# One decoder layer on one core: where the attention probabilities' word planes are split and joined, and in which order two weight chunks are multiplied

## The reference, cut to what matters

```
proj = h @ w_in                              # q, k, v of MoBA; q, k, v, r of GLA; a low-rank gate
p = softmax(q k^T * scale - slope * distance)          # MoBA, 8 heads x 64, causal, one block
moba_o = p @ v
o = chunked gated linear attention(qg, kg, vg, log_a)  # GLA, 4 heads, key 64, value 128
gla_o = rmsnorm(o) * gla_norm_g * silu(rg)             # rg: the output gate
mix = concat(moba_o, gla_o) @ w_mix_o
x = LN1(alpha * x + mix)
x = LN2(alpha * x + CrossAttn(x, mem))       # keys and values of mem from w_xkv
x = LN3(alpha * x + W2 relu(W1 x)^2)
```

## Time and profile before

| | us |
|---|---|
| median of 3 runs | 400.91 (400.53 to 401.12) |
| the profiled execution: its time | 399.95 |
| its span, first to last instruction | 398.0 |
| PE busy in the span | 387.2 (97%) |
| DVE busy | 354.3 (89%) |
| ACT busy | 260.3 (65%) |
| POOL busy | 100.4 (25%) |
| mean granted TensorE clock | 0.997 of full speed |

### The profile page before, as it was taken

One profiled execution on the slowest core, in us unless ns is written; L12 is line 12 of the kernel. 1 busy time (PEld: TensorE's weight loads), 2 busy tenths in 40 slices (PEclk: granted clock), 3 DMA queues, 4 the chain that ended last, 5 costly groups with the idle time before them and its releaser, 6 DMA issues.

```text
span 398.0 us, 5609 instructions
## 1 busy us (share of the span) xinstructions
PE 387.2 (97%) x2068; PEld 329.1 (83%) x2068; DVE 354.3 (89%) x450; ACT 260.3 (65%) x341; POOL 100.4 (25%) x87
## 2 busy tenths in 40 slices
PE   8999999978999999999999999999999999999995
PEld 5888888867888888898988888888888888888883
DVE  5599596999998787878798888999999999999997
ACT  6667578524745645547585548788877777888751
POOL 2059344856882202200102500000000000000003
PEclk9999999999999999999999999999999999999998
DMA  8997739493773274364818556767777777776202
GB/s 290 376 357 260 253 111 245 134 352 102 248 276 113 101 246 178 116 215 172 260 38 308 198 176 184 212 195 240 234 221 235 238 230 230 233 228 182 75 2 105
DMA packets 31585, 81.27 MB, mean 204 GB/s; under 512 B 8038, under 2 KB 9670, under 8 KB 27462
## 3 DMA queue, kind: packets, MB, share of 16 engines
q1 hardware_dynamic: 28720, 76.39, 57.1%
q0 software_dynamic: 2160, 3.93, 5.7%
q10 hardware_dynamic: 678, 0.59, 0.5%
HBM read 78.28 MB, written 1.05 MB: 199 GB/s over the span
## 4 chain that ended last, share of the span: by engine, by line
PE 69%; DVE 1%; issue 0%; DVEq 0%
PE bank L1705 14%; PE bank L1706 14%; PE bank L1707 13%; PE bank L2078 13%; PE bank L2085 7%; PE bank L1764 4%; PE bank L1768 2%; PE bank L1711 1%; PE bank L1891 1%; PE bank L1957 0%; PE bank L2006 0%; DVE stats L1650 0%; DVE X L1659 0%; PE bank L2164 0%; PE bank L1956 0%
## 5 line engine op out<-in xcount | busy, mean ns | idle before, releaser
L1110 DVE TENSOR_TENSOR w_lo<-raw,w_hi 128x2048 fp32r<-128x2048 f32 x30 | 72.7, 2430 | 5.9 <-ACT w_hi L692 5.9
L692 ACT CAST w_hi<-raw 128x2048 fp32r<-128x2048 f32 x32 | 60.7, 1912 | 16.2 <-PE bank L1707 11.1
L2078 PE MATMUL bank<-actA,w_hi 128*128 128x512 f32 x224 | 55.4, 390 | 0.0
L655 POOL DMA_DIRECT2D raw<-in_w_ff x15 | 13.2, 877 | 155.6 <-DMA raw<-in_w_ff 155.6
L2078 PEld LDWEIGHTS bank<-actA,w_hi 128*128 128x128 f32 x224 | 42.0, 188 | 8.7
L1705 PE MATMUL bank<-w_hi,actB 128*128 128x512 f32 x107 | 42.6, 398 | 0.0
L1706 PE MATMUL bank<-w_lo,actB 128*128 128x512 f32 x107 | 41.8, 391 | 0.0
L1707 PE MATMUL bank<-w_hi,actB 128*128 128x512 f32 x107 | 41.8, 390 | 0.0
L1764 PE MATMUL bank<-actA,w_hi 128*128 128x512 f32 x156 | 38.3, 392 | 0.0
L1705 PE MATMUL bank<-w_hi,actA 128*128 128x512 f32 x96 | 37.9, 395 | 0.0
L1707 PE MATMUL bank<-w_hi,actA 128*128 128x512 f32 x96 | 37.4, 390 | 0.0
(11 more groups left out here) (254 smaller groups left out, 889.1 us busy)
## 6 DMA issues: line engine op xcount, KB each, us to landing
raw<-in_w_ff SPq DMA_DIRECT2D x32, 1024.0 KB, 5.4
raw<-in_w_in SPq DMA_DIRECT2D x10, 1024.0 KB, 6.3
raw<-in_w_xkv SPq DMA_DIRECT2D x8, 1024.0 KB, 6.8
raw<-in_w_mix_o SPq DMA_DIRECT2D x4, 1024.0 KB, 4.9
raw<-in_w_xq SPq DMA_DIRECT2D x4, 1024.0 KB, 5.0
raw<-in_w_xo SPq DMA_DIRECT2D x4, 1024.0 KB, 5.5
raw<-in_w_ff POOLq DMA_DIRECT2D x15, 256.0 KB, 5.0
raw<-in_lead SPq DMA_DIRECT2D x6, 384.0 KB, 5.3
```

The costliest lines, as they stand in the source:

```text
L655: pool.dma_start(half_view(u)[:, 1536:2048], w_ff2[q, :, 512:1024], accum_op=ALU.add)\
L692: act.copy(dst, half_view(u)).then_inc(hi_done, 1)
L1110: dve.tensor_tensor(dst, half_view(u), hi_part.bitcast(f32), ALU.subtract).then_inc(lo_done, 1)
L2078: pe.matmul(b[:, :].rearrange("p (h s) -> p h s", h=2), hi[:, k, m * P:(m + 1) * P], actA[:, :, k, :], start=k == 0, stop=False, skip_grou ...
```

## The change

It has three parts.

1. POOL makes all four splits in a row, and the four joins move to ACT. SP issues the second, third and fourth turn directly behind each other, and unit (7, 0), unit (7, 1) and then X behind them; before, X stood behind the second turn and unit (7, 0) between the third and the fourth.
2. The output gate's columns become chunk 4 and GLA's values chunk 5. `rg0` and `rg1` are multiplied first. `exp_r(0)` stands between the exponentials of the softmax, `silu(0)` ahead of the last four norms on DVE; `silu(1)` keeps its place. `vg0` takes bank 5 as before and `vg1` bank 4 in place of 1.
3. On ACT the casts of both halves of chunk 5 stand in a row, and so do their low parts on DVE.

```
 CHUNKS = [ ...
-    ("w_in", "cols", VG), ("w_in", "cols", RG),
+    ("w_in", "cols", RG), ("w_in", "cols", VG),
 ...
-    + ... + [("va1", 4), ("vg0", 5), ("vg1", 1)]
-    + [("rg0", 2), ("diag", 0), ("rg1", 3), ("xk00", 0), ("xk01", 1), ("pv0", 6), ("pv1", 7)]
+    + ... + [("va1", 4)]
+    + [("rg0", 2), ("rg1", 3), ("vg0", 5), ("diag", 0), ("vg1", 4), ("xk00", 0), ("xk01", 1), ("pv0", 6), ("pv1", 7)]
 ...
-CHUNK_END = {..., 4: "vg1", 5: "rg1", ...}
+CHUNK_END = {..., 4: "rg1", 5: "vg1", ...}
 @@ sync
             load(unit(6, 0), chunk_source(6, 0), 4)
             turn_planes(0)
             load(unit(6, 1), chunk_source(6, 1), 4)
-            turn_planes(1)
+            for j in range(1, HA // 2):
+                turn_planes(j)
+            load_chunk(7)
             sp.dma_start(X[:], ...).then_inc(x_in, 16)
-            turn_planes(2)
-            load(unit(7, 0), chunk_source(7, 0), 4)
-            turn_planes(3)
-            load(unit(7, 1), chunk_source(7, 1), 4)
 @@ gpsimd
-            make_planes(0)
-            make_planes(1)
-            join_planes(0)
-            join_planes(1)
-            make_planes(2)
-            make_planes(3)
+            for j in range(HA // 2):
+                make_planes(j)
             wait_full(pool, "diag")
             pool.memset(lev_q[1], 0.0).then_inc(lev_q_zeroed, 1)
-            join_planes(2)
-            join_planes(3)
 @@ scalar
+            def join_planes(j):
+                act.wait_ge(turned_in[j], 16)
+                act.copy(by_word(planes[j]), by_plane(probs_words[j])).then_inc(probsT_made, 1)
 ...
             hi_half(5, 0)
-            evacuate("vg0", vg[:, 0, :])
+            hi_half(5, 1)
             exps(4)
             exps(5)
-            hi_half(5, 1)
+            exp_r(0)
             exps(6)
             exps(7)
-            evacuate("vg1", vg[:, 1, :])
+            exp_r(1)
             hi(MEM_UNIT, actB_hi[:].rearrange("p a s -> p (a s)"))
+            join_planes(0)
             hi_half(6, 0)
-            exp_r(0)
+            join_planes(1)
+            evacuate("vg0", vg[:, 0, :])
             b = wait_full(act, "diag")
             act.copy(diag[:], b[:, 0:8]).then_inc(freed("diag"), 1)
             hi_half(6, 1)
             decay(0)
-            exp_r(1)
+            join_planes(2)
+            evacuate("vg1", vg[:, 1, :])
+            join_planes(3)
+            decay(1)
             hi_half(7, 0)
-            decay(1)
             hi_half(7, 1)
 @@ vector
             lo_half(5, 0)
-            norm(4)
-            norm(5)
             lo_half(5, 1)
-            norm(6)
-            norm(7)
+            silu(0)
+            for h in range(4, HA):
+                norm(h)
 ...
             exponents(0)
             lo_half(6, 0)
             lo_half(6, 1)
-            silu(0)
             exponents(1)
             silu(1)
 @@ tensor
-            tokens(4, 0, A, "vg0")
-            tokens(4, 1, A, "vg1")
-            tokens(5, 0, A, "rg0")
+            tokens(4, 0, A, "rg0")
+            tokens(4, 1, A, "rg1")
+            tokens(5, 0, A, "vg0")
             b = begin("diag")
 ...
-            tokens(5, 1, A, "rg1")
+            tokens(5, 1, A, "vg1")
```

More of the change, by code:

```diff
@@ L168 @@
      ("ka0", 1), ("ka1", 2), ("ka2", 3), ("ka3", 0), ("va0", 2)]
-    + [(f"score{h}", b) for h, b in enumerate((4, 5, 6, 7, 1, 3, 0, 2))] + [("va1", 4), ("vg0", 5), ("vg1", 1)]
[1 row of a table removed]
+    + [(f"score{h}", b) for h, b in enumerate((4, 5, 6, 7, 1, 3, 0, 2))] + [("va1", 4)]
[1 row of a table added]
     + [("lv0", 4), ("lv1", 5), ("xk10", 2), ("xk11", 3), ("xk20", 0), ("lv2", 6), ("xk21", 1), ("lv3", 7),
@@ L184 @@
     FILL[_name] = (_bank, sum(b == _bank for b, _ in FILL.values()))
-CHUNK_END = {0: "kg1", 1: "qa3", 2: "ka3", 3: "va1", 4: "vg1", 5: "rg1", 6: "xk11", 7: "xk31", 8: "xv01",
+CHUNK_END = {0: "kg1", 1: "qa3", 2: "ka3", 3: "va1", 4: "rg1", 5: "vg1", 6: "xk11", 7: "xk31", 8: "xv01",
              10: "mo11", 11: "xv11", 12: "xq11", 13: "xq31", 15: "xo11", C_FF1_0: "hid1"}
@@ L579, in make_planes @@
                 pool.tensor_copy(by_plane(planes[j]), by_word(probs_words[j])).then_inc(planes_made, 1)
-            def join_planes(j):
-                pool.wait_ge(turned_in[j], 16)
-                pool.tensor_copy(by_word(planes[j]), by_plane(probs_words[j])).then_inc(probsT_made, 1)
-            make_planes(0)
-            make_planes(1)
-            join_planes(0)
-            join_planes(1)
-            make_planes(2)
-            make_planes(3)
+            for j in range(HA // 2):
+                make_planes(j)
             wait_full(pool, "diag")
             pool.memset(lev_q[1], 0.0).then_inc(lev_q_zeroed, 1)
-            join_planes(2)
-            join_planes(3)
             pool.wait_ge(lev_q_zeroed, 2)
@@ L755, in exps, with exp_r @@
                                    accum_out=sums[:, 2 * h + t:2 * h + t + 1]).then_inc(exp_done, 1)
+            def exp_r(t):
+                b = wait_full(act, f"rg{t}")
+                act.activation(sg[:, t, :], b[:, :], ACT.Exp, scale=-1.0).then_inc(expr_done, 1)
+            def join_planes(j):
+                act.wait_ge(turned_in[j], 16)
+                act.copy(by_word(planes[j]), by_plane(probs_words[j])).then_inc(probsT_made, 1)
             hi_half(4, 0)
@@ L765, in _ @@
             hi_half(5, 0)
-            evacuate("vg0", vg[:, 0, :])
+            hi_half(5, 1)
             exps(4)
             exps(5)
-            hi_half(5, 1)
+            exp_r(0)
             exps(6)
             exps(7)
-            evacuate("vg1", vg[:, 1, :])
+            exp_r(1)
             hi(MEM_UNIT, actB_hi[:].rearrange("p a s -> p (a s)"))
+            join_planes(0)
             hi_half(6, 0)
-            def exp_r(t):
-                b = wait_full(act, f"rg{t}")
-                act.activation(sg[:, t, :], b[:, :], ACT.Exp, scale=-1.0).then_inc(expr_done, 1)
-            exp_r(0)
+            join_planes(1)
+            evacuate("vg0", vg[:, 0, :])
             b = wait_full(act, "diag")
@@ L1201, in _, with silu @@
             lo_half(5, 0)
-            norm(4)
-            norm(5)
             lo_half(5, 1)
-            norm(6)
-            norm(7)
+            def silu(t):
+                dve.wait_ge(expr_done, t + 1)
+                v = sg[:, t, :]
+                link(dve.tensor_scalar(v, v, 1.0, None, ALU.add))
+                link(dve.reciprocal(v, v))
+                b = wait_full(dve, f"rg{t}")
+                dve.tensor_tensor(v, v, b[:, :], ALU.mult).then_inc(freed(f"rg{t}"), 1)
+            silu(0)
+            for h in range(4, HA):
+                norm(h)
             def exponents(n):
@@ L1256, in masked @@
                     b[:, :].rearrange("p (a b w) -> p a b w", a=8, w=w)).then_inc(freed(name), 1)
[L1258 to L1264, removed]
             def mix(n, name):
```

## The result

| | before | after |
|---|---|---|
| median | 400.88 us (400.53 to 401.12, 4 runs) | 395.03 us (394.53 to 395.20, 4 runs) |
| ratio, 95% interval | | 0.9853 (0.9836 to 0.9870) |
| profiled execution: time, span | 399.95, 398.0 us | 394.53, 392.6 us |
| its mean granted clock | 0.997 | 1.000 |

The account below looks back on a forecast made before the run. PE was taken to bound the kernel, with 4.8 us of waits before 102 us; 0.3 + 2.1 + 1.5 + 0.2 = 4.1, plus 0.2 for refills, gave 400.91 - 4.3 = 396.6 us, range 395.4 to 399.3.

Parts of the forecast that it names:

- What bounds it: PE bounds the kernel; its waits of 4.8 us before 102 us, plus some tenths for refills, are the most to gain.
- the first: Rival: all PE waits go, DVE gets its 4.4 us and locks back without new ones; 395.9 us, chance 0.13.
- the late turns of the others: Fourth turn late: rival 2, 7.6 us turn plus a lock, 398.6 us, chance 0.21; rival 4, far later, 402.8, 0.06.
- The last join: PE's 2.08 us wait for the last join before pv goes, with 2.9 us to spare.
- The size of a join: A join on ACT takes 1.4 us, from a cast's time by the element; the skill's estimate was 1.47 us.
- The lock: A POOL copy holds DVE for its length; moving joins gives DVE back about 1.9, 1.7 and 0.7 us.
- Level 1: PE's 1.54 us wait for POOL's part of level 1 goes, with 0.7 us to spare, the tightest place.
- The low parts: PE's wait for (6, 1) shrinks from 0.44 to 0.1 us, for (7, 1) from 0.73 to 0.5.
- The queue and X: X behind chunk 7 on SP delays chunk 8's units by 2.8 us, at no cost; X is read after 113.
- the banks: New banks for vg0 and vg1, read out later, cost nothing; 1.9 us of cover at the first.
- The waits and the refills: PE's waits give 0.3 + 2.1 + 1.5 + 0.2 = 4.1 us, pipeline refills beside them 0.2.
- The step that failed: Final step: the median's 0.96 us above the profiled execution is carried over, giving 400.91 - 4.3 = 396.6 us.

Follow-up runs that it names:

- the runs on one chip: The changed kernel again, unchanged, 394.93 us, and the kernel before with only part 1 of the change, 395.77 us, timed on the same chip.
- the changed kernel with the slow start: The changed kernel run once more, unchanged: 395.91 us, ratio 0.9855 to the kernel before.
- the second trace of the kernel before: Trace of the kernel before run once more, unchanged: 400.71 us, ratio 0.9990.
- the filled kernel: The kernel before with ten idle products between level 0 and level 1 on PE: 400.76 us, ratio 0.9991.

## Why the prediction was right in kind and short in size

- **What bounds it: right.** PE gained where it had waited, and after 102 us no new wait stands. Of the rivals the first came nearest in time (395.9), but by luck: its mechanism, all waits gone and no new lock, didn't come. A wait of 0.66 is left and both late splits met DVE's work. None of the late turns of the others came.
- **The last join: right.** The 2.08 us went, with 2.2 us of cover where 2.9 were forecast. The size of a join was wrong (1.95 us, not 1.4), which used only idle time of ACT. The estimate of 1.47 us from the Trainium skill was nearly as far off (ScalarE: Activation LUTs, "What ACT_TABLE_LOAD costs"); the page gives its figure for fp32 and bf16, and these are 16-bit integers.
- **The lock: right, and it is the whole matter.** With the joins on POOL the gain is zero. The fourth split met the subtraction as stepped through.
- **Level 1: right.** No wait is left, with 1.0 us to spare where 0.7 was forecast: `decay(1)` at 82.81, 84.3 forecast.
- **The low parts: right.** A wait of 0.66 us at 96.5, forecast 0.5 at 97.1 (the start is 0.8 earlier).
- **The queue and X: the cost of nothing was right**, and so was it for the banks.
- **Parts 2 and 3: small.** By the runs on one chip, 0.84 us on top of part 1, which gives the rest. The prediction didn't split them.
- **The waits and the refills.** Of the sum's terms the waits came as forecast, 4.13 us against 4.1. The refills were mis-sized: 0.5 us, not 0.2, with the three waits that went (0.44, 2.08 and 1.54).
- **The step that failed: "The median of the runs is 0.96 above that execution, so I forecast 400.91 - 4.3 = 396.6."** It takes the one traced execution for a typical one and carries its distance from the median over to the changed kernel. There the distance is 0.50 (395.03 - 394.53), and the traced execution also had the luck of a fast start. Of the miss of 1.57 us, 0.34 is the stretch (4.64 against 4.3, the refills), and the remaining 1.2 is this step.

Where the excess was, the marks show. A kernel's median less the mark to end of its trace is what stands ahead of the first mark and behind the last product. In 12 of the other 13 traces that is 45.0 to 45.6 us, and in one (the changed kernel with the slow start) 46.5. In the trace that the forecast was read from it is 46.75 (400.88 - 354.13), though its first mark at 39.59 is itself a late one. So this execution ran some 1.2 us faster between the marks than the kernel before usually does. It is an estimate, since it takes the other traces for typical. The excess lay in the stretch, and the change takes it away: by the second trace of the kernel before the stretch gains 5.60 us of the 5.85.

What it is made of, the runs show in part. In the execution traced first, PE's 4.8 us of waits came in pieces, the longest 2.08, and the clock held. In the second trace 4.12 of them came in one piece, the clock fell, and the stretch was 0.96 us longer. But most of the 0.96 was there before the fall: level 1 began at 92.2 us in both, though the second trace had passed the first mark 0.78 us earlier (38.81 against 39.59), so the fast start gained nothing there. What the fall cost behind it came mostly in place of the wait of 0.73 for the low part of (7, 1) and its refill, which the second trace doesn't have. Over the 71 executions of the kernel before in the three sets the mean granted clock is 0.989 to 0.999 with a mean of 0.993, lower than the 0.997 of the first trace in all but one; the changed kernel's 13 runs have 0.997 to 1.000. So the execution that I read was an unusual one by its clock too, and the change takes away the long waits behind the low clock. What stays open is how much of the median's excess is the clock. Over the 71 the time hardly follows the clock (those at 0.995 and above have a median of 401.06 us, those at 0.993 and below 400.98), and filling the wait raised the clock and not the speed. It may be that an execution without a fall pays in longer waits, as the traced one of the filled kernel did; that is argued, not shown.

## What to carry to other kernels

Here a copy on GpSimd beside a full VectorE cost VectorE its whole length, and on an engine with idle time it cost nothing, even at the same duration; look for such copies before moving products or transfers about. When the profiled execution is faster than the median and its mean clock higher than that of the other runs, it may not be a typical one: a gain worked out from it can leave out what waits cost in the others, and the range must reach below. Compare two traces from a mark behind the start, or chance at the start is read as gain.

## What the hardware did that I had not expected

**The start.** Nine warm-up products run first, identical in every kernel. Before:

```profile
0.76 4.00 PE L1756 MATMUL bank<-const-bfloat16-1.0 128*128 128x512 bf16 x9 [0.76 <-PEq L2190]
...
7.24 1.09 PE L1764 MATMUL bank<-actA,w_hi 128*128 128x512 f32 x4
```

After:

```profile
0.76 3.53 PE L1750 MATMUL bank<-const-bfloat16-1.0 128*128 128x512 bf16 x9 [0.76 <-PEq L2184]
...
6.44 1.12 PE L1758 MATMUL bank<-actA,w_hi 128*128 128x512 f32 x4
```

The row of nine lasted 3.50 to 4.00 us over the traces, and the first 512-column products began between 6.44 and 8.00 (the latter in a trace of the changed kernel). That is a spread of 1.5 us by chance, and at the first mark it is 2.16 (38.78 to 40.94). The clock column reads 1.00 in both stretches from 0 to 8 us, even where nine products take 4.00 us, 0.44 each, twice the 0.22 apiece that the same sort of product took in the filled kernel (2.13 us for nine). At the start the column doesn't show the speed that the durations show.

**The clock's fall.** After waits of 4.12, 3.80, 3.12 and 3.11 us PE came back at or near 0.50, the 1.2 GHz level, and in the two where I compared the same products this cost 1.7 us; after waits of 2.08 and 2.29 it stayed at 1.00. At the products behind it a wait of 4 us so cost some 40% more than its length; by the end of the kernel part of that had come in place of later waits.

**A 16-bit copy on ACT.** The joins, 1536 elements for each partition, take 1.95 us, as long as 2048 of fp32 (1.91).
